# Where the weight slots and the activation halves start in on-chip memory, modulo 128 bytes, in a kernel of four blocks on one core

## The reference

```python
proj = h @ w_in                       # every mixer; 1024 columns in, up to 7584 out
y = y * jax.nn.sigmoid(y @ w_glu + b_glu)
merged = gates[:, :, 0] * y_mla + gates[:, :, 1] * y_conv + gates[:, :, 2] * y_ret
x = x + rms_norm_2(merged @ w_out[l], ln_mix_post[l])
h = rms_norm_2(x, ln_ffn_pre[l])
f = (jax.nn.silu(h @ ffn_w_gate[l]) * (h @ ffn_w_up[l])) @ ffn_w_down[l]
x = x + rms_norm_2(f, ln_ffn_post[l])
```

## The kernel before

| tensor | before: address (mod 128, mod 256) | after: address (mod 128, mod 256) |
|---|---|---|
| `weights_raw`, `weights_lo` (share it) | 16512 (0, 128) | 16576 (64, 192) |
| `weights_hi` | 41088 (0, 128) | 41152 (64, 192) |
| `weights_hi_more` | 208320 (64, 192) | 208576 (64, 192) |
| `weights_raw_more`, `weights_lo_more` (share it) | 216512 (64, 192) | 216768 (64, 192) |
| `act_F_hi`, `act_F_lo` | 103936, 112128 (0, 0) | 104064, 112256 (0, 128) |
| `ffn_F_hi`, `ffn_F_lo` | 120320, 142848 (0, 0) | 120448, 142976 (0, 128) |
| `mla_F_hi`, `mla_F_lo` | 122400, 126496 (32, 32) | 122624, 126720 (0, 0) |
| `conv_F_hi`, `conv_F_lo` | 192832, 196928 (64, 64) | 193152, 197248 (0, 128) |
| `hn_F` (rows of the first stage) | 57472 (0, 128) | 57536 (64, 192) |
| `x_T`, `h_T`, `gains`, `junk` | (64, 192) | (0, 0) |

## Time and profile before

### The profile page before, as it was taken

One profiled execution on the slowest core, in us unless ns is written; L12 is line 12 of the kernel. 1 busy time (PEld: TensorE's weight loads), 2 busy tenths in 40 slices (PEclk: granted clock), 3 DMA queues, 4 the chain that ended last, 5 costly groups with the idle time before them and its releaser, 6 DMA issues.

```text
span 1253.8 us, 19035 instructions
## 1 busy us (share of the span) xinstructions
PE 1223.1 (98%) x7597; PEld 1024.5 (82%) x7597; DVE 902.0 (72%) x1463; ACT 638.7 (51%) x1034; POOL 101.0 (8%) x163
## 2 busy tenths in 40 slices
PE   7999999999999999999999999999999999999998
PEld 3566778888978878787999987988788787999986
DVE  7998877667688987687555645489998687566553
ACT  4344555675547664545443544556565545444441
POOL 6300011101000200201000002000200201000000
PEclk9999999999999999999999999999999999999999
DMA  7636566445565546355666565565445355655552
GB/s 256 210 92 187 187 216 191 151 120 166 159 184 166 155 153 197 120 166 183 204 186 186 186 188 160 165 211 158 162 152 187 129 167 168 191 185 186 186 191 74
DMA packets 71958, 215.68 MB, mean 172 GB/s; under 512 B 16256, under 2 KB 19744, under 8 KB 71744
## 3 DMA queue, kind: packets, MB, share of 16 engines
q1 hardware_dynamic: 65008, 206.37, 51.9%
q0 software_dynamic: 2112, 6.97, 1.8%
q10 hardware_dynamic: 4752, 1.14, 0.4%
HBM read 208.95 MB, written 3.15 MB: 169 GB/s over the span
## 4 chain that ended last, share of the span: by engine, by line
PE 85%; DVE 8%; ACT 3%; issue 2%; POOL 1%; DMA 0%; DVEq 0%; POOLq 0%; ACTq 0%
PE acc L696 17%; PE acc L698 17%; PE acc L697 17%; PE acc L675 8%; PE acc L674 8%; PE acc L676 8%; PE acc L635 3%; PE mixed L1011 1%; DVE weights_lo L1772 1%; ACT junk L1275 1%; PE mixed L1108 1%; PE turned L751 1%; DVE h_T L1802 1%; PE mixed L995 1%; PE mixed L1004 1%
## 5 line engine op out<-in xcount | busy, mean ns | idle before, releaser
L1772 DVE TENSOR_TENSOR weights_lo<-weights_raw,weights_hi 128x1024 fp32r<-128x1024 f32 (+1 forms) x304 | 355.8, 1205 | 72.0 <-ACT weights_hi L1240 71.4
L1240 ACT ACTIVATE weights_hi<-weights_raw 128x1024 fp32r<-128x1024 f32 (+1 forms) x304 | 305.2, 1043 | 77.5 <-DMA weights_raw<-stream_dram 77.2
L696 PE MATMUL acc<-weights_hi,act_F_hi 128*128 128x512 f32 (+1 forms) x680 | 275.6, 405 | 5.2 <-DVE act_F_lo L1802 3.4
L698 PE MATMUL acc<-weights_hi,act_F_lo 128*128 128x512 f32 (+1 forms) x680 | 267.3, 393 | 0.0
L697 PE MATMUL acc<-weights_lo,act_F_hi 128*128 128x512 f32 (+1 forms) x680 | 267.2, 393 | 0.0
L674 PE MATMUL acc<-act_F_hi,weights_hi 128*128 128x256 f32 x624 | 177.1, 284 | 0.0
L676 PE MATMUL acc<-act_F_lo,weights_hi 128*128 128x256 f32 x624 | 175.8, 282 | 0.0
L675 PE MATMUL acc<-act_F_hi,weights_lo 128*128 128x256 f32 x624 | 175.7, 282 | 0.0
L696 PEld LDWEIGHTS acc<-weights_hi,act_F_hi 128*128 128x128 f32 x680 | 128.0, 188 | 36.5 <-DVE act_F_lo L1802 4.3
L698 PEld LDWEIGHTS acc<-weights_hi,act_F_lo 128*128 128x128 f32 x680 | 127.9, 188 | 29.2
L697 PEld LDWEIGHTS acc<-weights_lo,act_F_hi 128*128 128x128 f32 x680 | 128.2, 189 | 26.7
(11 more groups left out here) (339 smaller groups left out, 1928.4 us busy)
## 6 DMA issues: line engine op xcount, KB each, us to landing
weights_raw<-stream_dram SPq DMA_DIRECT2D x306, 512.0 KB, 3.6
weights_raw_more<-stream_dram SPq DMA_DIRECT2D x58, 512.0 KB, 3.6
gains<-rows_dram POOLq DMA_DIRECT2D x12, 512.0 KB, 4.8
weights_raw<-stream_dram SPq DMA_DIRECT2D x6, 416.0 KB, 3.2
weights_raw<-stream_dram SPq DMA_DIRECT2D x4, 384.0 KB, 3.9
x_T<-x_in_dram SPq DMA_DIRECT2D x4, 256.0 KB, 5.9
ssm_bc<-ssm_bc_dram SPq DMA_DIRECT2D x1, 1024.0 KB, 8.4
u_scratch<-u_T ACTq DMA_DIRECT2D x4, 256.0 KB, 5.8
```

Of the source, the lines that this page charges most:

```text
L696: pe.matmul(o, xh, wh, start=first and kk == 0, stop=False)
L698: i = pe.matmul(o, xl, wh, start=False, stop=last and kk == s["nk"] - 1)
L1240: act.activation(high(s, slice(0, n)), whole(s, slice(0, n)), ACT.Copy).then_inc(hi_made, 1)
L1772: dve.tensor_tensor(low(s, slice(0, n)), whole(s, slice(0, n)), high(s, slice(0, n)).bitcast(F32), ALU.subtract).then_inc(lo_made, 1)
```

## The change

Four unused tensors are put into the list of allocations and one placeholder grows by 32 bytes. No instruction is added, removed or moved on any engine; what changes is only where operands lie (the table above). Weights in places 0 to 5 go from residue 0 to 64 modulo 128; those in places 6 and 7 stay at 64. All rows' halves come to a multiple of 128, where `act_F` and `ffn_F` already were.

```diff
+        sb("weights_offset", [P, 16])
         with ExitStack() as s0:
             sb("weights_near", [P, R0, SLOT], F32, s0)
...
+        sb("rows_offset", [P, 16])
         with ExitStack() as s0:
             toep = sb("toeplitz", [P, 2, SUB, PCOLS], F32, s0)
         f_hi = sb("act_F_hi", [P, DT, SEQ], F32R)
...
             cfp = sb("conv_params", [P, 4, TAPS + 3], F32, s4)
+            sb("latent_rows_offset", [P, 24], F32, s4)
             mo_hi = sb("mla_F_hi", [P, 4, SEQ], F32R, s4)
...
             with ExitStack() as s6:
+                sb("conv_rows_offset", [P, 24], F32, s6)
                 cf_hi = sb("conv_F_hi", [P, 4, SEQ], F32R, s6)
...
-                sb("mla_heads", [P, 3872], F32, s6)
+                sb("mla_heads", [P, 3880], F32, s6)
```

## The result

The changed kernel takes 1237.32 us (median of 4, 1235.79 to 1238.27) against 1256.15 of the kernel before on the same chip: ratio 0.9853, 95% interval 0.984 to 0.9865, so 18.8 us less. That is outside the predicted range. The profiled execution took 1237.6 us itself.

A forecast was written before the change was run, and what follows sets the result against it. TensorE's pace of starting matmuls was taken as the bound. Terms -1.8 + 0.4 + 1.6 + 0.4 = +0.6 us on the profiled 1255.56 gave 1256.2, 1257.2 us as median; 8-in-10 range 1249.2 to 1260.5, the case's own 1252.5 to 1258.0.

The forecast's parts named there:

- The step that failed: All fp32r products: the pace of places 6 and 7, 117.7 and 233.3 ns, was taken for all places.
- 256-wide in places 0 to 5: 1872 matmuls with stationary weights, feed-forward for example: pace from 118.7 to 117.7 ns, -1.8 us.
- 512-wide with `act_F`: 1968 matmuls with moving weights, places 0 to 5: pace from 232.5 to 233.3 ns, +1.6 us.
- with `ffn_F`: 432 512-wide matmuls, places 0 to 5, as in `down`: pace from 232.4 to 233.3 ns, +0.4 us.
- `conv_o`: 96 512-wide matmuls with `conv_F`: loses its good placement, 229.2 to 233.3 ns, +0.4 us.
- Places 6 and 7: Matmuls of both widths with weights there: residues modulo 128 are kept, so 0 us.
- `mla_F`: Its products' halves go from 32 to 0; no pair at one placement, so taken as 0, 0.2 us either way.
- Rival 1: All fp32r matmuls: the operands' distance modulo 256 counts; -9.3 us 512-wide, +2.9 us 256-wide, net -6.4, 1250.2 us; chance 0.28.
- Rivals 2: 256-wide matmuls fall into their slow rhythm of 120.0 ns; +6.3 us in all, 1262.9 us; chance 0.14.
- 3 (beyond 208 KB): Places 6 and 7 were fast 256-wide by lying beyond 208 KB; only 512-wide terms remain, +2.4, 1259.0 us; chance 0.12.
- 4 (placement does nothing): All matmuls: pace differences belong to rhythms alone, so 1256.6 us; chance 0.06.
- The rule of the Trainium skill: TensorE's reads: placement of multiples of 64 bytes is worth nothing, so the sum would be 0; given little weight.

The follow-up runs named there:

- the third kernel: Changed kernel with all rows' halves 128 bytes further, so weights' address minus rows', modulo 256 (D), is 192 everywhere; 1252.52 us, ratio 0.9985.

## Why the prediction was wrong

**What bounds the kernel: right.** TensorE's pace was the limit before and is after; the waits stayed small (1.8 and 2.2 us for the split weights), and every microsecond gained is a difference of pace. The engine went on at its own pace where hardly anything else ran, too. A window of the kernel before, near its end, has no VectorE work and no DMA:

```profile
1236.00:1243.00 7.00, 7.00 (x32) 5.67 (x31) 0.00 (x0) 0.51 (x2) 0.00 (x0) 1.00 0.00 0
```

Matmuls start there at 1236.02 and, 30 later, at 1242.98: 232.0 ns each, near the 232.4 of the earlier trace rows. So the extra nanoseconds of this form are no contention with VectorE or the DMAs; that they follow the distance of TensorE's own two operands points at its reads of them.

**The step that failed** is "Places 6 and 7 before have just the residues modulo 128 that all places get ... I take their pace for all". These places differ from 0 to 5 in two things at once, the residue of the weights and the distance to the rows (192 against 128 modulo 256), and the prediction took the first for the cause. Where the residues changed without the distance, nothing moved (1255.38 us); where places kept the forecast's residues with D at 192, the forecast's paces came true, 117.8 and 233.3 ns, and the profiled execution took 1255.46 where the sum said 1256.2. The arithmetic held for that execution; the rule didn't. The median there, 1252.52, is 4.7 below the forecast's 1257.2, since six of the ten executions belong to the lower group, which no trace explains. The prediction named this condition itself ("or the distance of the operands, for then the pair ... is no pair").

**Term by term.** 256-wide in places 0 to 5: -1.8 us forecast, -9.8 by the paces measured. 512-wide with `act_F`: +1.6 against -6.7; with `ffn_F`: +0.4 against -1.5. `conv_o`: +0.4 against 0: it kept D = 64, though its residues changed. Places 6 and 7: 0 against -4.0, for "keep their residues modulo 128" was true and beside the point. `mla_F`, VectorE, the taps, the first stage: 0, and measured as that; line 1776 has a median of 1218 ns as in the earlier trace rows, the taps 477 against 479:

```profile
L1776 DVE TENSOR_TENSOR weights_lo<-weights_raw,weights_hi x304: 682/1218/1228, 110.7 to 1213.7; 128x1024 fp32r<-128x1024 f32 x145, 128x832 fp32r<-128x832 f32 x3, 128x768 fp32r<-128x768 f32 x2, 128x512 fp32r<-128x512 f32 x2
...
L1806 DVE SCALAR_TENSOR_TENSOR conv_acc_F<-conv_in_F,conv_params,conv_acc_F x240: 468/477/486, 377.0 to 947.1; 128x256 f32<-128x256 f32 x120
```

**The rivals.** Rival 1 had the mechanism: the distance modulo 256. Its 512-wide price was right (229 ns, -9.3 us forecast, -9.5 measured). Its 256-wide price had the wrong sign, +2.9 against -12.5: it counted moving minus stationary and took for the 256-wide form what the 512-wide one pays at that value. In that form weights and rows have changed roles, and its map is its own: 64, counted weights minus rows, is its good distance, and no row of before had it, so neither sign could be read there. Had the rival left that price open between -(118.7 - 106.7) and the worst row, its range would have held the result. Rivals 2 (120.0 ns), 3 (beyond 208 KB) and 4 (placement does nothing) fell; 3 by the third kernel, where places 0 to 5 go at 117.8 too.

**The rule of the Trainium skill** that was weighed (page "SBUF — State Buffer", section "Who interferes with whom": two independent read ports, TensorE waits on no one) would have made the sum 0. The runs disagree: the distance of the two operands is worth up to 6.6 ns of a 256-wide matmul (119.9 against 113.3) and 7.2 of a 512-wide one (233.9 against 226.7). It was right to give it little; it would have been right to draw from the disagreement that the two reads may not be independent, and to weigh a rule about their relation above one about each.

**Worth of the parts.** `rows_offset` alone gives 1237.25 us; `weights_offset` alone 1255.38. What `weights_offset` and the `mla_heads` placeholder add to the one line is places 6 and 7 in the 512-wide form, 336 x 3.7 = 1.2 us by the paces and 1.0 by the times, within what a measurement tells from nothing.

**Still open.** That reads collide at all is argued from D and not seen. Which two it would be (a matmul's own pair, or the load of the next stationary operand with the stream that runs) wasn't separated: the kernel with only the low rows moved slowed all three lines. Nor is it shown what starts or ends the fast rhythm of the 256-wide form, and whether a distance other than 192 would keep it too; why some executions of the D = 192 kernel take 3.5 us less; or when the clock falls.

## What to carry to other kernels

Where TensorE is the bound and its matmuls follow each other without a wait, read its pace as starts over count for each pair of tensors, and compare with columns over the clock; if some nanoseconds are over, look at the distance of the two operands' start addresses modulo 256 before anything else, and for each form apart. One dummy allocation between the weights and the activations is a whole experiment: it gave 1.5% here. And where two cases of a trace differ in pace, list everything in which they differ, relations included, before taking one of these for the rule; a price for a placement that no row has belongs in the range, down to the bound of the columns themselves.

## What the runs showed of the hardware that was not expected

- fp32r matmuls of 128 x 128 by 512 columns start at best every 226.7 to 226.8 ns, and of 256 columns every 113.3. That is 17/16 of 213.3 and 106.7, the columns at 2.4 GHz; no stretch of any kernel here went below it in its mean.
- What comes on top is of about the same size for either width: 2.3 ns (229.0) to 7.2 (233.9) for 512 columns, and 4.5 (117.8) to 6.7 (120.0) for 256. So it doesn't look like a share of the stream; what it is no run tests.
- The same placement can have two paces in the 256-wide form: 113.3 and 117.8 at D = 64 as at D = 192, by what ran before; 118.7 and 120.0 at D = 128. A pace read at one spot is not yet the pace of a placement.
- In the middle of the kernel the granted clock fell to 1.2 GHz eight times in six of the fourteen profiled executions, seven times for 3.4 us and once for 6.8, each time in or just after a wait of TensorE of 0.75 or 1.87 us; the others had the same waits and no fall. A fall of 3.4 us costs about 1.7 us, a tenth of the whole gain.
